# The last combine stage of a two-layer decoder trunk as a phase of its own, with heads two tiles ahead and rows turned by transposing DMAs

## The reference

```
gates, y0, y1 = ...                      # the two experts' outputs of each token and their gates
h2  = h + g0 * y0 + g1 * y1              # the residual add of the mixture
x   = rmsnorm(h2, g_ple)                 # 4096 x 1024
h3  = h2 + sigmoid(x @ w_ple_gate) * (p[1] @ w_ple_up)     # w_ple_gate 1024 x 1024, w_ple_up 256 x 1024
out = rmsnorm(h3, g_final)
```

## Time and profile before

| | before |
|---|---|
| Median of 3 runs | 5489.29 us (5483.73 to 5489.83) |
| The profiled execution: time, and its span from first to last instruction | 5481.81 us, 5479.8 us |
| Mean granted TensorE clock | 0.938 of full speed |
| Last combine: its first DMA (a gain) is issued at | 4923.18 us |
| Last combine: end of its weight block, start of its loop | some 4946 us |
| Last combine: end of the span | 5479.8 us |

### The profile page before, as it was taken

One profiled execution on the slowest core, in us unless ns is written; L12 is line 12 of the kernel. 1 busy time (PEld: TensorE's weight loads), 2 busy tenths in 40 slices (PEclk: granted clock), 3 DMA queues, 4 the chain that ended last, 5 costly groups with the idle time before them and its releaser, 6 DMA issues. The chain is left out here.

```text
span 5479.8 us, 90667 instructions
## 1 busy us (share of the span) xinstructions
PE 4717.2 (86%) x29473; PEld 2996.9 (55%) x29893; DVE 2947.2 (54%) x5970; ACT 1945.8 (36%) x2841; POOL 1559.3 (28%) x1159
## 2 busy tenths in 40 slices
PE   7928999999938999998588888845999999986898
PEld 6916766666623444443355555524766676653444
DVE  5664444444444544443577777773444444435665
ACT  6714444433322122221344444413434344322232
POOL 1114444443401111110232333304444344322232
PEclk9959999999969999999799999967999999998999
DMA  6729999998945555553555555518999999854443
GB/s 219 273 96 316 308 308 302 302 295 285 288 139 143 147 146 143 153 146 93 130 146 153 149 148 151 140 46 277 307 309 304 297 310 282 289 162 150 146 137 114
DMA packets 1163421, 1129.77 MB, mean 206 GB/s; under 512 B 859984, under 2 KB 871248, under 8 KB 1163344
## 3 DMA queue, kind: packets, MB, share of 16 engines
q1 hardware_dynamic: 1117264, 961.02, 57.8%
q0 software_dynamic: 46080, 167.79, 9.4%
HBM read 695.58 MB, written 227.54 MB: 168 GB/s over the span
## 5 line engine op out<-in xcount | busy, mean ns | idle before, releaser
L724 POOL TENSOR_TENSOR ex_w_lo<-ex_raw,ex_w_hi 128x2048 bf16<-128x2048 f32 x192 | 779.2, 4085 | 1161.8 <-ACT ex_w_hi L778 1161.8
L778 ACT ACTIVATE ex_w_hi<-ex_raw 128x2048 bf16<-128x2048 f32 x384 | 707.3, 1900 | 523.4 <-PE ex_ps_y L110 187.9
L875 PE MATMUL ex_ps_gate<-ex_xT,ex_w_hi 128*128 128x0 bf16 x2048 | 572.3, 280 | 161.6 <-DMA ex_xT<-ex_xrow 126.3
L876 PE MATMUL ex_ps_gate<-ex_xT,ex_w_hi 128*128 128x0 bf16 x2048 | 572.1, 280 | 0.0
L877 PE MATMUL ex_ps_gate<-ex_xT,ex_w_lo 128*128 128x0 bf16 x2048 | 571.6, 279 | 0.0
L875 PE MATMUL ex_ps_up<-ex_xT,ex_w_hi 128*128 128x0 bf16 x2048 | 558.6, 273 | 0.0
L876 PE MATMUL ex_ps_up<-ex_xT,ex_w_hi 128*128 128x0 bf16 x2048 | 558.3, 273 | 0.0
L877 PE MATMUL ex_ps_up<-ex_xT,ex_w_lo 128*128 128x0 bf16 x2048 | 558.1, 273 | 0.0
L857 DVE COPY ex_y<-ex_ps_y 128x512 f32 x324 | 224.1, 692 | 566.5 <-PE ex_ps_y L110 515.6
L841 DVE TENSOR_TENSOR ex_aT<-ex_silu,ex_ps_up 128x384 bf16<-128x384 f32 x256 | 141.8, 554 | 719.6 <-PE ex_ps_up L877 538.2
L109 PE MATMUL ex_ps_y<-ex_w_lo,ex_aT 128*128 128x512 bf16 x1296 | 492.2, 380 | 8.5
(11 more groups left out here) (310 smaller groups left out, 9071.8 us busy)
## 6 DMA issues: line engine op xcount, KB each, us to landing
ex_raw<-in_w_exp_gate SPq DMA_DIRECT2D x128, 1024.0 KB, 11.1
ex_raw<-in_w_exp_up SPq DMA_DIRECT2D x128, 1024.0 KB, 13.8
ex_raw<-in_w_exp_down SPq DMA_DIRECT2D x128, 1024.0 KB, 5.8
y_rows<-ex_y SPq DMA_DIRECT2D x162, 512.0 KB
cb_hin<-h_mid SPq DMA_DIRECT2D x64, 512.0 KB, 4.7
mix_x<-in_x SPq DMA_DIRECT2D x32, 512.0 KB, 4.6
h_mid<-mix_h SPq DMA_DIRECT2D x32, 512.0 KB, 5.2
y_rows<-mix_zeros SPq DMA_DIRECT2D x32, 512.0 KB, 5.9
```

The lines of the kernel that those rows point to most:

```text
L724: eng.tensor_tensor(w_lo[u][:, w], raw[:, c, :], w_hi[u][:, w], ALU.subtract).then_inc(lo_done, 1)
L778: act.activation(w_hi[u][:, c * WCHUNK:(c + 1) * WCHUNK], raw[:, c, :], ACT.Copy).then_inc(hi_done, 1)
L875: pe.matmul(out, hi, x_hi, start=j == 0, stop=False)
L876: pe.matmul(out, hi, x_lo, start=False, stop=False)
```

## The change

Layer 0 keeps `combine_phase`, now without the branches of layer 1. Layer 1 gets `final_phase`, one block in which the following differs from before.

- The weights are loaded and split inside the block. Each of the ten chunks has a buffer and a semaphore. SP issues loads of tiles 0 and 1, then the ten chunks and `g_final`; ACT and DVE split them between the head of tile 0 and that of tile 1, after a wait for both the gain and `g_final`. PE starts when the eight chunks of the gate weight are done.
- Step s has the load of tile s+4, the head of tile s+2, the middle of tile s and the tail of tile s-1. `h2`, `xT` and `pT` are rings of four, `x` and `ph` have two buffers. The loop body holds four steps.
- `x` and `ph` are turned by two transposing DMAs that SP issues. PE has no transposes, DVE no copies from PSUM.
- PE's step is gate(0), up(0), gate(1), up(1). ACT and DVE do the head's pieces between those of the middle, in the order shown.

Its core (declarations, and the parts that repeat the old ones with other indices, are left out):

```diff
-def combine_phase(nc, A, C, layer, out):
+def combine_phase(nc, A, C, layer):
...
+def final_phase(nc, A, C, layer, out):
+    RING = 4
...
+        raw = [m.sb(f"raw{n}", [P, D]) for n in range(len(jobs))]
+        h2 = [m.sb(f"h2_{r}", [P, D]) for r in range(RING)]
+        x = [m.sb(f"x{u}", [P, 2, D], BF16) for u in (0, 1)]
+        ph = [m.sb(f"ph{u}", [P, 2, PLE], BF16) for u in (0, 1)]
+        xT = [m.sb(f"xT{r}", [P, 2, KD, P], BF16) for r in range(RING)]
+        pT = [m.sb(f"pT{r}", [P, 2, KPLE, P], BF16) for r in range(RING)]
...
+        def steps(eng, step, weights):
+            for s in range(-4, -1):
+                step(s, s % RING)
+            weights()
+            for s in range(-1, RING):
+                step(s, s % RING)
+            with eng.Fori(1, NT // RING - 1) as i:
+                for r in range(RING):
+                    step(RING * i + r, r)
+            for s in range(NT - RING, NT + 1):
+                step(s, s % RING)
...
+            def step(s, r):                                     # SP
+                u = r % 2
+                if has(s + 4):
+                    t = s + 4
+                    wait(sp, h2_done, t - 1)
+                    sp.dma_start(hin[u][:], h_t[t]).then_inc(h_ld[u], 16)
+                    wait(sp, pl_done, t - 1)
+                    sp.dma_start(p_in[u][:], p_t[t]).then_inc(p_ld[u], 16)
+                if isinstance(s, int) and s == -3:
+                    for n, (w, k, _, _, _) in enumerate(jobs):
+                        sp.dma_start(raw[n][:], w[k * P:(k + 1) * P, :]).then_inc(w_loaded[n], 16)
+                    sp.dma_start(g_final[:], row(A["g_final"])).then_inc(gain_loaded, 16)
+                if has(s - 1):
+                    sp.wait_ge(o_done, s)
+                    sp.dma_start(out_t[s - 1], o_out[1 - u][:]).then_inc(o_st[1 - u], 16)
+                if has(s + 2):
+                    t = s + 2
+                    q = (r + 2) % RING
+                    sp.wait_ge(pl_done, t + 1)
+                    sp.sem_inc(turn_open, 1)
+                    if not isinstance(t, int) or t >= RING:
+                        sp.wait_ge(gate_mm, 2 * (s - 1))
+                        sp.sem_inc(turn_open, 1)
+                        sp.wait_ge(up_mm, 2 * (s - 1))
+                        sp.sem_inc(turn_open, 1)
+                    sp.dma_start(pT[q][:]..., ph[u][:]..., transpose=True).then_inc(turned[u], 16)
+                    sp.wait_ge(xl_done, t + 1)
+                    sp.sem_inc(turn_open, 1)
+                    sp.dma_start(xT[q][:]..., x[u][:]..., transpose=True).then_inc(turned[u], 16)
...
+            def weights():                                      # ACT; DVE has the same, after w_hi_done
+                act.wait_ge(gain_loaded, 32)
+                for n, (_, _, gain, hi, _) in enumerate(jobs):
+                    act.wait_ge(w_loaded[n], 16)
+                    act.activation(hi, raw[n][:], ACT.Copy, ...).then_inc(w_hi_done, 1)
...
+            # POOL's step: rs3(s-1); rs2(s+2); slot(s+4) and its two gathers, after h2(s+2)
+            # ACT's step: squares(h3, s-1); ph hi(s+2); squares(h2, s+2); tanh 0(s); x hi(s+2); tanh 1(s)
+            # DVE's step: h2(s+2) in two; ph lo(s+2); ms3(s-1); ms2(s+2); o_out(s-1); x lo(s+2);
+            #             mid 0, h3 0, mid 1, h3 1 of s
...
+            def weights():                                      # PE
+                pe.wait_ge(w_lo_done, KD)
+            def step(s, r):
+                if has(s):
+                    pe.wait_ge(turned[r % 2], 2 * done(s, r % 2))
+                    for h in (0, 1):
+                        c = slice(512 * h, 512 * h + 512)
+                        wait(pe, th_done, 2 * s + h - 1)
+                        product(ps_gate[h][:], xT[r], wg, KD, c).then_inc(gate_mm, 1)
+                        if isinstance(s, int) and s == 0 and h == 0:
+                            pe.wait_ge(w_lo_done, KD + KPLE)
+                        wait(pe, mid_done, 2 * s + h - 1)
+                        product(ps_up[h][:], pT[r], wu, KPLE, c).then_inc(up_mm, 1)
...
-                experts_phase(nc, A, C, 1), lambda: combine_phase(nc, A, C, 1, out)]
+                experts_phase(nc, A, C, 1), lambda: final_phase(nc, A, C, 1, out)]
```

More of the change, by code:

```diff
@@ L1066, in combine_phase @@
         ss2, ms2, rs2, ss3, ms3, rs3 = (m.sb(n, [P, 1]) for n in ("ss2", "ms2", "rs2", "ss3", "ms3", "rs3"))
[L1067 to L1078, removed]
+        x3 = m.sb("x3", [P, 2, D], BF16)
+        x3T = m.sb("x3T", [P, 2, KD, P], BF16)
+        ra = m.sb("ra", [P, 512])
+        rb = m.sb("rb", [P, 512])
+        q_out = m.sb("q_out", [P, D])
+        kv_out = m.sb("kv_out", [P, 2 * KVW])
         ps = [m.ps(f"b{i}", [P, 512]) for i in range(5)]
@@ L1122, in step @@
                 v = 1 - u
-                if tail and qkv:
+                if tail:
                     t = s - 1
@@ L1136, in step @@
                     sp.dma_start(p_in[u][:], p_t[t]).then_inc(p_ld[u], 16)
-                if head and qkv:
+                if head:
                     t = s + 1
@@ L1158, in step @@
                     sp.dma_start(kv_t[t], kv_out[:]).then_inc(q_st, 16)
[L1159 to L1162, removed]
             steps(sp, step)
[L1165 to L1171, removed]
+            sp.wait_ge(q_st, 32 * NT)
+            for u in (0, 1):
+                sp.wait_ge(h3_st[u], 8 * NT)
         @block.gpsimd
@@ L1280, in step @@
                     dve.tensor_scalar(ms2[:], ss2[:], 1.0 / D, EPS, ALU.mult, ALU.add).then_inc(ms2_done, 1)
[L1281 to L1286, removed]
                 if head:
@@ L1308, in residual @@
                                              op0=ALU.mult, op1=ALU.add).then_inc(h3_done, 1)
-                if head and not qkv:
-                    take_x(s + 1)
                 if mid_:
-                    if qkv:
-                        wait(dve, h3_st[u], done(s - 2, u) if not isinstance(s, int) or s >= 2 else 0)
+                    wait(dve, h3_st[u], done(s - 2, u) if not isinstance(s, int) or s >= 2 else 0)
                     residual(0)
-                if mid_:
                     residual(1)
-                if mid_:
                     dve.wait_ge(ss3_done, s + 1)
@@ L1355, in up @@
                     c = slice(512 * h, 512 * h + 512)
-                    if qkv and h == 0:
+                    if h == 0:
                         wait(pe, rot_mul, 3 * (s - 2) + 3)
@@ L1360, in up @@
                     product(ps_up[h][:], pT[u], wu, KPLE, c).then_inc(up_mm, 1)
[L1362 to L1374, removed]
-                if mid_:
[L1377 to L1380, removed]
-                        pe.wait_ge(xT_done, s + 1)
-                        pe.wait_ge(pT_done, s + 1)
+                if mid_:
+                    pe.wait_ge(x_turned, 16 * s + 16)
+                    pe.wait_ge(p_turned, 16 * s + 16)
                     gate(0)
-                    if qkv:
-                        up(0)
+                    up(0)
                     gate(1)
-                    if qkv:
-                        up(1)
-                if head and not qkv:
-                    turn_head()
-                if mid_ and not qkv:
-                    up(0)
                     up(1)
-                if tail and qkv:
+                if tail:
                     t = s - 1
```

234 lines of the change are left out of this document (191 added, 43 removed).

## The result

The changed kernel takes 5405.6 us, the median of four runs (5402.2 to 5414.2); the kernel before, measured beside it, took 5489.6 us (median of four, 5483.7 to 5490.4). The ratio is 0.985, its 95% interval 0.984 to 0.986: 84 us less. The forecast was 5398, its range 5386 to 5430. The profiled execution took 5406.4 us with a span of 5404.7 us (before: 5481.8 us, span 5479.8 us) at a clock of 0.937.

A forecast was written before the change was run, and what follows sets the result against it. The prediction took PE's serial stream, with the head's chain ending in its middle, as the bound. PE's 502.0 us become 2.5 + 32 x 12.95 = 416.9 (-85.1), start -5.8, end 0: -90.9, from 5489.3 to 5398.4 us; range 5386 to 5430.

The forecast's parts named there:

- PE-bound loop at 12.95 us: Last combine's loop: without gap and transposes a tile costs PE's 60 matmuls, 12.95 us, 2.74 us less for 32 tiles.
- DVE hidden: Last combine's loop: DVE's work for a tile takes 11.5 us and stays under PE's 12.95.
- The wait for `g_final`: Start: ACT and DVE touch no chunk before `g_final` lands at 4951; PE starts at 4962, not 4967.8: -5.8 us.
- DMA at 10.3 us a tile, and a turn of 4.3 us: Loop: plain 6.8 plus turned 3.5 us of DMA engine time in 12.95, 80%; transposing DMA lands 4.3 us after issue.
- "It just fits" for tile 1: Start: tile 1's rows are turned at 4976, and PE ends tile 0 at 4977.5.
- Two signs that the prediction named as showing it wrong: PE idle before gate(0) with the transposing DMA as releaser; a clock of 0.5 after the start.
- The rival of the start (5407): Overlap at the start gains nothing or loses: PE starts at 4967, tile 1 late by 3 us; no separate chance.
- The end: After the last up product the same instructions follow, 10.0 us, unchanged.
- The DMA-bound rival (5442): Loop: all 2.88 MB a tile at 201 GB/s, period 14.3 us, 43 us more; forecast to this, 5408 to 5470: 0.15.
- the slower one (5521): Loop: transposing DMAs slow all that travels with them, 172 GB/s, 16.8 us a tile, 123 us over forecast; chance 0.04.
- The rival of blocks turned one after the other: Loop: each of 20 blocks costs its own latency; slower kernel from 16.5 us a tile, 5512; chance 0.01.
- The row on prices by kind: DMA engine time from layer 0 and last combine: 3.1 us per 1000 KB plain, 5.4 turned.

The follow-up runs named there:

- the version with the gain apart: Changed kernel with `g_final` on its own semaphore, so splitting the weights waits for the small gain alone; 5396.5 us, ratio 0.9835.

## Why the prediction was right

The mechanism of the loop was the forecast one, and the size within 8 us (5405.6 for 5398). By the steps of the prediction:

- **PE-bound loop at 12.95 us: right.** Measured 12.95, PE busy for 100 of 100 us. The run with the turns left on PE splits the gain in 1.60 us a tile for the lead and 1.14 for the transposes; the prediction treated them as one. The run without the lead shows that the second part alone would have been a loss.
- **DVE hidden: right.** It waits 2.0 us a tile for PE before the second `mid`.
- **The wait for `g_final`: right.** ACT was forecast 27.8 us after S (4951 - 4923.2) and came after 28.2; the first gate product after 38.8 and came after 39.2. The rate was 376 GB/s over the 28.2 us (380 taken), for 10.6 MB (10.2 taken). From ACT's start to the first product it took 11.0 us (11.1 forecast) with some luck: ACT's eight chunks took 8.4 us, not 9.8, and DVE ended 2.5 us behind it, not 1.3.

```profile
4930.47:4958.69 28.22, 0.00 (x0) 0.00 (x0) 4.34 (x5) 2.71 (x4) 6.92 (x10) 0.50 0.98 376
```
```profile
4959.94 9.65 DVE L1521 SCALAR_TENSOR_TENSOR cb_wg<-cb_raw,cb_g_ple,cb_wg 128x1024 bf16<-128x1024 f32 x8 [12.37 <-ACT cb_wg L1482]
```

- **DMA at 10.3 us a tile, and a turn of 4.3 us: too low, and this is the step that failed.** The tile showed a share of 1.08, 14.0 us of 12.95, and a turn took 10.3. I had priced plain and turned bytes each by itself, and added. The price is right where they do not meet: with the gathers held the share is 0.81, 10.5 us. What was missing is the term for their meeting, 3.5 us of engine time a tile and 6 us of landing. The 11 us of cover absorbed it in the loop.
- **"It just fits" for tile 1: wrong, by the same term.** Tile 1 was forecast turned 1.5 us before PE needs it, on a landing of 4.3 us. It came late by 6.2 us, and the second cold start came on top, eight matmuls at the lower clock, some 1.7 us: 425.1 us from first product to last `mid` instead of 416.9, 8.2 us more. That is half of what the profile lies above the sum: the stage took 82.4 us less than before where 90.9 were forecast, 8.2 in the filling and 0.4 at the start; the rest, 7.3 us, is the later beginning of the stage (4930.5 for 4923.2), which comes from the phases ahead. 5390.9 + 8.2 + 0.4 + 7.3 = 5406.8, against 5406.4 measured. Two signs that the prediction named as showing it wrong were there, for this one tile: PE idle before a gate product with the turning DMA as releaser, and a clock of 0.5 after the start.
- **The rival of the start (5407)** comes nearest in time. It was right that tile 1 is late, and wrong that PE starts at 4967: PE started 39.2 us after S, as forecast, and the lateness came from the turn alone.
- **The end: right.** 10.0 us.
- **The DMA-bound rival (5442) and the slower one (5521)** named the right resource, but took the rate of a short, full stretch for a bound. In the loop a share of 1.07 to 1.09 at 218 to 225 GB/s stood beside a PE that never waited. The share counts the time of the packets, and it fell to 0.81 for the same bytes in another order, so a share above 1 does not say that a period is too short for its bytes.
- **The rival of blocks turned one after the other: wrong.** The 16 blocks of a tile landed in a median of 4.2 to 4.3 us in the loops whose turns had no gather beside them (no gathers, gathers held, one tile ahead). Gathers are not all that can delay a turn: tile 0's, issued while the weights were still being loaded, took some 9.7 us also in the run without gathers, where none was in flight. The Trainium skill's advice for TensorE ("VectorE: DVE Perf Modes", Rules for kernel authors) holds for the order of before, where the DMA version is 0.6% slower, and not with a lead of two tiles, where it is 31 us faster (5437.4 to 5405.9); by the profiles 11 of these us are the later start of the version that turns on PE.

The row on prices by kind also stands after the runs. Without the gathers a tile is 1152 KB plain and 640 KB turned in 0.54 x 12.95 = 7.0 us; less 3.6 us for the plain part at 3.1 per 1000 KB, the turned part is 3.4 us, 5.3 per 1000 KB, against the 5.4 forecast. Over a longer stretch, 5000 to 5350, the share is 0.52, which makes it 4.9. The Trainium skill, "Advanced Engine Details and Errata", section X-Bar Transpose (TRN2), has the two kinds equally fast; these runs do not bear it out.

Open is why the two kinds hinder each other. That both queues lose time is shown; whether in the engines, the memory or the order of the packets no run here tells. Nothing of it reached the loop's time, which PE set in both orders. Nor was it tried to hold the plain loads of `hin` and `p` apart from the turns.

## What to carry to other kernels

When work moves from a busy engine to a DMA, ask first how far ahead the result is made: one tile of lead made this DMA turn a loss, two made it free. Price a DMA not by its bytes alone but by what flies with it, and check the price at the filling of the pipeline, where there is no lead yet. A wait that orders a gather behind a turn cost nothing here and brought the start back. And look for a late load that shares a semaphore with early ones: `g_final` held up the splitting of the weights by 10.6 us.

## What was not expected of the hardware

- A turning DMA and gathers in flight together take more engine time than one after the other: 1.09 against 0.81 of the engines for 21.8 and 22.8 MB in 100 us, landing 10.3 against 4.3 us for the turn and 7.3 against 5.5 for the gather.
- The issue of the turning DMA of x held SP's queue longer where the engines were fuller: a median of 1.8 us in the loop without gathers (share 0.54), 3.7 us in that of the changed kernel (1.08), and there 7.6, 3.7 and 11.9 us for the first three tiles (rows of the last two below). Loads of the next tile stand behind it.

```profile
4979.01 3.71 SPq L1440 DMA_TRANSPOSE cb_xT<-cb_x  x1
...
4987.76 11.92 SPq L1440 DMA_TRANSPOSE cb_xT<-cb_x  x1
```

- After 6.2 us of idle, behind 15 us of work on tile 0, the granted clock was at its lower level (0.75 on average at 4985 to 4990, 0.57 in the next 5 us), and eight matmuls ran at half speed. The same came of 2.4 us of idle before tile 1 and again before tile 2 in the version with the gain apart (eight matmuls each), and of 4.6 us in the version with one tile of lead (7 to 14 matmuls). The 1.6 us of idle before tile 2 in the repeat of the changed kernel left the clock up.
